# One block from the merge to the experts, and another order of the routing work in a decoder layer on one Trainium2 core

## The reference, cut to what matters

```python
gates = jax.nn.sigmoid(proj[..., OFF_GATE:IN_COLS]).reshape(B, T, N_BRANCH, D)
merged = gates[:, :, 0] * y_a + gates[:, :, 1] * y_b + gates[:, :, 2] * y_c
h = layer_norm(ALPHA * x + merged @ prm['w_out'], prm['ln1_g'], prm['ln1_b'], LN_EPS)
...
scores = jax.nn.sigmoid((xt @ prm['w_router']).astype(jnp.float32))
_, idx = lax.top_k(scores + prm['b_router'].astype(jnp.float32), TOP_K)
sel = jnp.take_along_axis(scores, idx, axis=-1)
gate = sel / jnp.sum(sel, axis=-1, keepdims=True) * ROUTED_SCALE
...
h = jax.nn.silu(xb @ prm['w_e1'][e]) * (xb @ prm['w_e3'][e])
yb = (h @ prm['w_e2'][e]).astype(jnp.float32) * w[:, None]
...
y = layer_norm(ALPHA * h + moe_ffn(h, prm), prm['ln2_g'], prm['ln2_b'], LN_EPS)
```

## Time and profile before

| | us |
|---|---|
| median of 3 runs | 2023.21 (2018.51 to 2024.14) |
| the profiled execution, its own time | 2027.02 |
| its span | 2025.3 |
| TensorE busy | 1784.4 (88%) |
| VectorE busy | 632.6 (31%) |
| ScalarE busy | 389.1 (19%) |
| GpSimd busy | 362.4 (18%) |

### The profile page before, as it was taken

How to read it: one execution, slowest core, us unless ns; L and a number is a source line. 1 busy time by engine, 2 the same in 40 slices (tenths; PEclk the granted TensorE clock), 3 DMA queues, 4 the chain that set the end, 5 groups by cost and what they waited for, 6 DMA issues and landing times. The chain is left out here.

```text
span 2025.3 us, 29331 instructions
## 1 busy us (share of the span) xinstructions
PE 1784.4 (88%) x10614; PEld 1052.9 (52%) x10614; DVE 632.6 (31%) x1516; ACT 389.1 (19%) x916; POOL 362.4 (18%) x529
## 2 busy tenths in 40 slices
PE   7999997879999998899988978888787878888887
PEld 6857776778778884465533333333333333333332
DVE  1387754774214311431111111111111111111127
ACT  0114544442120100211111111111111111111102
POOL 1000001888870000001111011111111111011100
PEclk8999998999999999999999899999999999899898
DMA  4433312001242324269999999999999999999976
GB/s 118 145 138 104 105 32 48 3 21 36 60 152 80 113 81 187 106 252 402 420 421 419 408 418 407 410 419 405 410 399 409 405 404 406 392 409 417 404 294 251
DMA packets 160782, 532.04 MB, mean 263 GB/s; under 512 B 22061, under 2 KB 88927, under 8 KB 110205
## 3 DMA queue, kind: packets, MB, share of 16 engines
q1 hardware_dynamic: 138971, 488.63, 61.3%
q0 software_dynamic: 20640, 41.23, 5.4%
q10 hardware_dynamic: 1098, 1.18, 0.2%
HBM read 522.52 MB, written 41.42 MB: 278 GB/s over the span
## 5 line engine op out<-in xcount | busy, mean ns | idle before, releaser
L1965 PE MATMUL bank<-arena 128*64 128x512 f32 x2048 | 504.7, 650 | 146.3 <-DMA arena<-in_w_e 146.3
L1965 PEld LDWEIGHTS bank<-arena 128*64 128x64 f32 x2048 | 157.6, 149 | 488.9 <-issue 488.9
L1983 PE MATMUL bank<-arena 128*64 128x512 f32 x1024 | 233.8, 598 | 0.0
L2212 DVE TENSOR_TENSOR arena<-bank,arena 128x256 f32<-128x256 f32 x64 | 27.2, 425 | 578.4 <-ACT arena L2057 578.4
L1835 POOL DMA_INDIRECT arena<-h_rows,index x66 | 66.9, 1013 | 776.5 <-DVE index L2087 727.6
L1425 PE MATMUL bank<-arena 128*128 128x276 f32 x768 | 183.0, 397 | 7.3 <-ACT arena L1527 3.1
L1425 PEld LDWEIGHTS bank<-arena 128*128 128x128 f32 x768 | 145.3, 190 | 41.1 <-ACT arena L1527 3.5
L1201 PE MATMUL bank<-arena 64*64 64x64 f32 (+2 forms) x2816 | 124.2, 243 | 28.5 <-DVE arena L1314 15.3
L2057 ACT ACTIVATE arena<-bank 128x256 f32<-128x256 f32 x64 | 24.7, 385 | 603.9 <-PE bank L1965 603.9
L1201 PEld LDWEIGHTS bank<-arena 64*64 64x64 f32 x2816 | 109.3, 138 | 35.3 <-DVE arena L1314 16.2
L1983 PEld LDWEIGHTS bank<-arena 128*64 128x64 f32 x1024 | 67.8, 136 | 110.9 <-issue 109.7
(11 more groups left out here) (332 smaller groups left out, 1850.0 us busy)
## 6 DMA issues: line engine op xcount, KB each, us to landing
arena<-in_w_e SPq DMA_DIRECT2D x384, 1024.0 KB, 14.0
arena<-in_w_in SPq DMA_DIRECT2D x50, 512.0 KB, 4.1
arena<-routed_rows SPq DMA_DIRECT2D x8, 2048.0 KB, 22.9
arena<-in_w_mem_kv SPq DMA_DIRECT2D x4, 1024.0 KB, 5.9
arena<-in_cache_mem_k SPq DMA_DIRECT2D x8, 512.0 KB, 5.1
arena<-in_cache_mem_v SPq DMA_DIRECT2D x8, 512.0 KB, 6.6
arena<-in_w_out SPq DMA_DIRECT2D x2, 2048.0 KB, 13.0
arena<-in_w_s SPq DMA_DIRECT2D x3, 1024.0 KB, 10.6
```

The costliest lines, as they stand in the source:

```text
L1965: mm = pe.matmul(p_gu[t * S:(t + 1) * S, :], xt[:, v, c, t * S:(t + 1) * S], w13[2 * v + t][:, :, c, :], start=(c == 0), stop=(c == KD - 1))
L1983: mm = pe.matmul(p_y[h][t * S:(t + 1) * S, :], hidT[:, j, t * S:(t + 1) * S], w2[2 * v + t][:, j, h * 512:(h + 1) * 512], start=(j == 0), ...
```

## The change

The merge stage, its `recycle`, and the mix and experts stage become one block, `stage_wkv_to_experts`: `stage_mix_experts` turns into `mix_programs`, which returns five programs that are called behind those of the merge. In place of the barrier stand waits: DVE counts a column tile of `merged` in the third pass (`tile_merged`), TensorE's first projection product waits for each column tile as it comes to it, POOL waits for all eight before it loads residual rows, and each engine waits for what it needs from the old stage. In the mix, ACT copies the turned rows of the tile before, and DVE picks the top eight of tile i-2, ahead of the next norm (`norm` is split into `mean` and `norm`, with `weigh` between them); the first two halves of the shared expert's first piece move up between the last routing products, and the second piece moves up too.

```diff
@@ merge_programs, vector
-            if x:
+            if x == 1:
                 dve.tensor_tensor(dst, dst, gtmp, ALU.add)
                 dve.drain()
+            if x == 2:
+                dve.tensor_tensor(dst, dst, gtmp, ALU.add).then_inc(sem("tile_merged"), 1)
+                dve.drain()
@@ mix_programs, gpsimd
                 .then_inc(sem("ln1_loaded"), 16)

+        pool.wait_ge(sem("tile_merged"), KD)
         for i, (c0, n) in enumerate(TILES):
@@ mix_programs, tensor
             for k in ks:
+                if i == 0:
+                    pe.wait_ge(sem("tile_merged"), k + 1)
                 for h in range(2):
...
         route(NTT - 2)
+        pe.wait_ge(sem("shared_loaded"), 32)
+        pe.wait_ge(s_mean, NTT - 1)
+        shared(0, 0)
         turn_h(NTT - 1)
         route(NTT - 1)
+        shared(1, 0)
...
-            pe.wait_ge(sem("shared_loaded"), 32)
             pe.wait_ge(s_mean, NTT)
-            shared(0, 0)
-            find_slots(0, 0, 0)
-            shared(1, 0)
-            find_slots(1, 1, 1)
             pe.wait_ge(s_rc, NTT - 1)
             shared(0, 1)
+            find_slots(0, 0, 0)
+            shared(1, 1)
+            find_slots(1, 1, 1)
             count = rounds(pe)
             pe.wait_ge(s_in[0], 16)
             turn(0)
-            shared(1, 1)
             pe.wait_ge(s_sa, 1)
@@ mix_programs, scalar
         for i in range(NTT):
-                if i == NTT - 1:
+            if i >= 2:
                 scores(i - 2)
+            if i >= 1:
+                copy_h(i - 1)
             square(i)
-                if i < NTT - 1:
-                    if i >= 1:
-                        copy_h(i - 1)
             root(i)
-                    if i >= 2:
-                        scores(i - 2)
-                else:
-                    root(i)
-                    copy_h(i - 1)
@@ mix_programs, vector
-            norm(0)
-            norm(1)
-            for i in range(2, NTT):
-                if i == NTT - 1:
+        for i in range(NTT):
+            if i >= 2:
                 pick(i - 2)
+            mean(i)
+            if i >= 2:
                 weigh(i - 2)
             norm(i)
-                if i < NTT - 1:
-                    pick(i - 2)
-                    weigh(i - 2)
@@ the new stage
+def stage_wkv_to_experts(nc, m, io):
+    wkv_sync, wkv_gpsimd, wkv_tensor, wkv_scalar, wkv_vector = wkv_programs(m, io)
+    merge_sync, merge_tensor, merge_scalar, merge_vector = merge_programs(m, io)
+    mix_sync, mix_gpsimd, mix_tensor, mix_scalar, mix_vector = mix_programs(m, io)
+    s_written, s_merged, s_sig = m.sem("outputs_written"), m.sem("tile_merged"), m.sem("gates_ready")
+    with nc.Block() as block:
+        @block.sync
+        def _(sp):
+            wkv_sync(sp)
+            merge_sync(sp)
+            mix_sync(sp)
+
+        @block.gpsimd
+        def _(pool):
+            wkv_gpsimd(pool)
+            pool.wait_ge(m.sem("rwkv_ready"), 1)
+            pool.wait_ge(s_written, 16 * OUT_WKV)
+            mix_gpsimd(pool)
+
+        @block.tensor
+        def _(pe):
+            wkv_tensor(pe)
+            merge_tensor(pe)
+            pe.wait_ge(s_sig, 3 * KD - 1)
+            mix_tensor(pe)
+
+        @block.scalar
+        def _(act):
+            wkv_scalar(act)
+            merge_scalar(act)
+            act.wait_ge(s_written, 16 * OUT_WKV)
+            mix_scalar(act)
+
+        @block.vector
+        def _(dve):
+            wkv_vector(dve)
+            merge_vector(dve)
+            dve.wait_ge(s_written, 16 * OUT_WKV)
+            dve.wait_ge(m.sem("sample_states_out"), 16 * 16)
+            mix_vector(dve)
@@ build
-            if stage is stage_wkv_merge:
-                m.recycle(WKV_ONLY)
```

More of the change, by code:

```diff
@@ L1634, in merge_programs @@
     return sync, tensor, scalar, vector
[L1637 to L1665, removed]
 O_WOUT = O_TOP
@@ L1888, in shared_half @@
-            def shared_half(x, j, first, bank):
-                for k in range(KD):
-                    mm = pe.matmul(m.ps[bank][:, x * THIRD:(x + 1) * THIRD], ws[x][:, k, j * P:(j + 1) * P],
-                                   m.arena[:, ds(first + O_HT + k * NT, THIRD)], start=(k == 0), stop=(k == KD - 1))
-                return mm
-            def shared(x, g):
-                j, third, bank = EARLY_GROUPS[g]
-                mm = shared_half(x, j, third * THIRD, bank)
-                if x == 1:
-                    mm.then_inc(s_sh, 1)
@@ L2020, in copy_turned @@
-            def copy_turned(g, v):
-                act.wait_ge(s_t, g + 3)
-                for x in range(2):
-                    last = act.activation(xt[:, v, 4 * x:4 * x + 4, :], p_turn[x][:, :].rearrange("p (c s) -> p c s", c=4), ACT.Copy)
-                last.then_inc(s_xt, 1)
-            for i in range(NTT):
-                if i == NTT - 1:
-                    scores(i - 2)
-                square(i)
-                if i < NTT - 1:
-                    if i >= 1:
-                        copy_h(i - 1)
-                    root(i)
-                    if i >= 2:
-                        scores(i - 2)
-                else:
-                    root(i)
-                    copy_h(i - 1)
@@ L2155, in _ @@
-            dve.memset(counts[:, 0, :], 0.0)
-            dve.tensor_scalar(rows8, m.row[:, :], float(TOPK), -1.0 - FAR, ALU.mult, ALU.add)
-            for i in range(NTT):
-                dve.tensor_scalar(info[:, i, 0:NE, 0], m.ones[:, :], m.row[:, i:i + 1], -FAR, ALU.mult, ALU.add)
-            dve.wait_ge(sem("score_zeroed"), 1)
-            dve.wait_ge(sem("ln1_loaded"), 32)
-            dve.wait_ge(sem("router_bias_loaded"), 16)
-            norm(0)
-            norm(1)
-            for i in range(2, NTT):
-                if i == NTT - 1:
-                    pick(i - 2)
-                    weigh(i - 2)
-                norm(i)
-                if i < NTT - 1:
-                    pick(i - 2)
-                    weigh(i - 2)
@@ L2172, in _ @@
-            dve.sem_inc(s_yv, 1)
-            dve.sem_inc(s_idx, 1)
-            pick(NTT - 2)
-            weigh(NTT - 2)
-            pick(NTT - 1)
-            weigh(NTT - 1)
-            dve.wait_ge(s_pos, 1)
-            dve.tensor_tensor(place[:, 0:4, 0:NE], m.ps[4][:, :].rearrange("p (a n) -> p a n", a=4), rest[:, 0:4, :], ALU.add)
-            dve.wait_ge(s_pos, 2)
-            dve.tensor_tensor(place[:, 4, 0:NE], m.ps[5][:, 0:NE], rest[:, 4, :], ALU.add)
-            dve.drain()
-            one_hot(0, 0)
@@ L2192, in _ @@
-            dve.drain()
-            dve.tensor_reduce(more, top8[:, 0, 0:MAX_ROUNDS - 1], AX.X, ALU.add)
-            dve.drain()
-            dve.tensor_scalar(m.rounds[:, :], more, 1.0, None, ALU.add).then_inc(s_rounds, 1)
-            slots_out(1, 1)
-            shared_product(0, 0, third(0), 3)
-            shared_product(1, 0, third(1), 7)
-            def shared_samples():
-                dve.drain()
-                for j in range(2):
-                    dve.tensor_copy(ssam[:, j, :].rearrange("p (b t) -> p b t", b=BS), sample_cols(sact[:, j, SEQ:NT]))
```

733 lines of the change are left out of this document (411 added, 322 removed).

## The result

| | before | changed |
|---|---|---|
| median of 7 runs, us | 2023.21 (2018.51 to 2026.68) | 2011.83 (2009.03 to 2019.09) |
| span of the profiled execution, us | 2025.3 | 2010.1 |

The ratio of the changed kernel's times to those of before is 0.9945, with a 95% interval of 0.9927 to 0.9963: 11.4 us less at the medians (7.5 to 14.8 by the interval), where 16.1 were forecast. The measured time lies inside the range, but the forecast gain of 16.1 lies above the interval.

The account below looks back on a forecast made before the run. The prediction took DMA transfers of expert weights to bound the loop, so only its start could move. Gains of 8.6 and 7.5 us, 16.1 together, took the median from 2023.2 to 2007 us, range 2001 to 2015.

Parts of the forecast that it names:

- The bound: Expert loop: weight transfers set its pace, so its length stays and every microsecond of earlier start comes off the end.
- Part one: Boundary between merge and projection: removing the barriers gains 6.1 us of idle time and 2.5 of clock, 8.6 together.
- The covers: First projection: residual rows land 4 us before DVE needs them; DVE's 1.2 us table set-up lies beside the first product.
- Part two: Last tiles up to the loop: the new order starts the first loop product 7.5 us earlier.
- at 870, before the gather: Last rows' store, behind 6.3 MB of weights on SP's queue, is through before POOL's first gather, at no cost.
- The bound given for this case, 2.1 us: If the store lands only when all that traffic is over, at 875, the loop starts 2.1 us later.
- at most 1.5: Short TensorE pauses before the loop may cost some clock, 1.5 us at most.
- (a): Rival: the last tiles' gain fails through a slow clock from tile 3's routing to the first slots; 2014.6 us, chance 0.13.
- (b): Rival: the loop starts earlier but its mean rate is 1% lower, giving back 10.5 us; 2018 us, chance 0.06.
- (c): Rival: gathers and scatters meet the weights in another phase, loop 1.8% longer, 19 us; 2026 us, chance 0.03.
- (d): Rival: the loop's mean rate comes out 0.5% higher, 5 us more gain; 2002 us and lower, chance 0.05.
- the rule on table switches: Each ACT table switch adds a 1.38 us drain; in the last tile about 1.6 us of gain would go, 2009 us.

Follow-up runs that it names:

- e8: Changed kernel, but the first projection product waits once for all eight column tiles; first loop product over 111.6 us after the merge, against 109.0.
- e2: Kernel before, keeping its barriers, with only the new orders of TensorE, ACT and DVE; ratio to before 0.9995 (0.9982 to 1.0009).
- e7: Changed kernel with SP issuing the last rows' store before the weights of experts 0 and 1; first gather at 90.5 us after the merge, against 93.9.
- e9: Changed kernel with the last rows' store issued by ACT instead of SP; first gather at 90.4 us after the merge, against 93.9.
- e3: Changed kernel with the second norm's parameter loads moved behind the second gather's landing; first gather at 94.5 us after the merge, against 93.9.
- e4: Changed kernel with ten idle TensorE products before the first turn and four behind it; first loop product over at 106.7 us after the merge, against 109.0.
- e13: The changed kernel once more, unaltered, on another comparison's chip; median 2016.17 us, ratio to before 0.9950 (0.9932 to 0.9968).
- e5: Changed kernel with POOL's gather-buffer fills from HBM replaced by a memset and two one-row loads; first gather at 93.0 us after the merge, against 93.9.
- e10: e9 with six idle TensorE products ahead of the first turn and four behind it; median 2011.85 us, ratio to before 0.9931.
- e1: Changed kernel's single block with the orders of TensorE, ACT and DVE as before; ratio to before 0.996 (0.9947 to 0.9974).

## Why the prediction was right, and where it was 4.7 us off

**The bound.** Right. The loop's length from the end of its first product to the start of its last is 1042.1 to 1045.5 us in fourteen profiles, 1042.1 to 1043.6 in thirteen of them, whatever the head did (it is 1043.5 before and 1043.2 changed). The head's gain arrives at the end in full. That the medians differ by nearly the profiles' 11.5 us is in part chance: the interval runs from 7.5 to 14.8.

**Part one, 8.6 us.** Right: 6.3 us of gap (6.11 to -0.16) and 2.5 of clock (30.17 to 27.63), 8.8 together. The covers held: the residual rows were issued at 772.20 and took 3.8 to 4.6 us (6.3 to 7.0 were taken over), the first product's mean begins at 783.98, and the table set-up lay beside that product. That the wait by column tile costs nothing and earns about 1.9 us is e8's 2.05.

**Part two, up to the first slots.** Right, 1.0 us on the safe side: the roundings of seven steps, the largest of them the place products (2.6 us without their wait, where 3.0 were taken over) and 0.2 more from part one.

**Part two, from the slots to the loop.** Of part two's 7.5 us only 2.7 arrived (11.5 less part one's 8.8); alone, in e2, it is worth 2.3 us in the profile and nothing that the runs can tell from zero. Here two terms were mis-sized. The first is the sentence that the last rows' store is through "at 870, before the gather". It was computed as all bytes ahead of it, divided by the rate, and came out 3 us ahead of the gather (88.6 us against 91.6 on the scale of the table). It let the gather go at 93.9, 17.3 us after its issue. The bound given for this case, 2.1 us, was the right one to fear: the gather came 2.3 us later than forecast. e7 and e9 show that it is this store and its place in the queue. The trace of before could have warned. Its last load of experts 0 and 1 (L1355, 854 to 856 us) is issued at 854.44:

```profile
DMA to landing us min/median/max: 17.3/17.3/17.3
```

It lands at 871.7, 19.8 us after the first was issued, where 7.3 MB at 425 GB/s are 17.2. In the changed kernel's form this takes 21.6 to 22.4 us (e3, e4, e13), with the fills issued early in between, and 18.7 without them (e5).

The second is the clock at this place, which the sum had at nothing and the bounds at "at most 1.5". The bound was taken from two rows of the loop, one pause of 1.01 us with no loss and one of 5.32 with 1.46. The same loop held worse, in its timeline:

```profile
1297.00 9.90 PE L1965 MATMUL bank<-arena 128*64 128x512 f32 x32 [3.37 <-DMA arena<-in_w_e]
```

That is 2.8 us lost behind a shorter pause. In the changed kernel the turn lost 0.9 us and the product 1.4, 2.3 in all (e4 gives just these back), in e9 2.9 for the product alone (9.97 against 7.09). Nor did the two rows cover a pause that is followed by a short piece of work and another pause.

Together 2.4 us at the turn, 0.9 in it and 1.4 in the product: 4.7 of 16.1, and 11.4 is what was measured. Of the rivals, (a) had the right effect in the wrong place: the clock did fall, but before the turn and not in the routing, and at a price of 2.3 us instead of 7.8. By the median alone (a)'s 2014.6 is nearer to the measured 2011.8 than the forecast 2007; it is the profile, with the slots 14.8 us earlier than before, that speaks against (a). (b), (c) and (d) did not occur. By the rule on table switches that the prediction quotes (the Trainium skill, "ScalarE: Activation LUTs", section "What ACT_TABLE_LOAD costs") 1.6 us would have gone before the slots; these came 1.0 us early. The timeline of the changed kernel, last tile:

```profile
843.52 1.28 ACT L1976 ACT_TABLE_LOAD   x1
...
844.82 0.20 ACT L1976 ACTIVATE arena<-arena 40x1 f32<-40x1 f32 x1
```

The root begins 0.02 us behind the load: nothing of a drain is to be seen after the change either.

What stays open: why the weights' last pieces, with the store's behind them, come 2 to 4 us after the bulk of the traffic (the thin rest in e3's windows), what sets the clock's price from profile to profile, and how e10's longer loop came about.

## What to carry to other kernels

The barriers between two stages cost 6.1 us here and, with them, 2.5 us of TensorE's clock; as the stage behind was bound by TensorE, both came back when the programs were joined, and the feeding of partial results added only the one last operation it hides (2 us). When a chain is shortened, look at every wait that was hidden behind it, and ask on which queue the thing stands: a small store behind 6.3 MB of prefetches held its reader until 1.8 us after they had landed, and on another queue it held nobody up. A price of the clock is not read from the length of one pause; where it matters, put work into the pause (here work that was there anyway, the shared expert's half) and measure.

## What was unexpected of the hardware

- A GpSimd memset of 128 x 2048 floats (1.80 us) held up a VectorE operation of 0.19 us until it was over (1.48 us).
- After pauses of TensorE of the same length, 3.2 us, the loop's product takes 7.09 us in some cases (changed kernel, at 1298.40) and 8.7 (before, at 1920.70) to 10.0 (e1, at 1274.49) in others; the first loop product took 8.45 to 9.97 us behind a slow turn and a pause of 1.2, and 7.09 wherever the pauses were filled.
- The loop of 64 pairs takes 1042.1 to 1043.6 us in thirteen of fourteen profiles, while whole runs of one kernel spread by 5.6 to 13.8 us. In these profiles the spread comes mostly from elsewhere: the merge ends at 769.1 to 776.1 us, and from the start of the loop's last product to the end it is 87.6 to 90.2.
